# Second copies of the split keys by transfers inside SBUF, and VectorE's splits one step behind ScalarE's

## The reference, cut to what matters

```python
ks = partial_rope(ks, pos); kw = partial_rope(kw, pos)
s = einsum('bgrqd,bgkd->bgrqk', q, k) * HEAD_DIM ** -0.5      # k is ks, then kw
p = softmax(where(kpos <= qpos, s, -inf)); o = einsum('bgrqk,bgkd->bgrqd', p, v)
o_n = g[..., 0:1] * o_c + g[..., 1:2] * o_s + g[..., 2:3] * o_w
```

## Time and profile before

| | us |
|---|---|
| median of 3 runs | 2821.78 (2821.71 to 2824.16) |
| profiled execution, its own time | 2825.9 |
| its span, first to last instruction | 2824.1 |
| PE busy in the span | 2725.4 (97%) |
| DVE busy | 1525.5 (54%) |
| ACT busy | 1156.0 (41%) |
| POOL busy | 229.0 (8%) |

### The profile page before, as it was taken

One profiled execution on the slowest core, in us unless ns is written; L12 is line 12 of the kernel. 1 busy time (PEld: TensorE's weight loads), 2 busy tenths in 40 slices (PEclk: granted clock), 3 DMA queues, 4 the chain that ended last, 5 costly groups with the idle time before them and its releaser, 6 DMA issues.

```text
span 2824.1 us, 34777 instructions
## 1 busy us (share of the span) xinstructions
PE 2725.4 (97%) x13497; PEld 2246.0 (80%) x13497; DVE 1525.5 (54%) x2678; ACT 1156.0 (41%) x2076; POOL 229.0 (8%) x322
## 2 busy tenths in 40 slices
PE   8899999999999999989999999999989899999997
PEld 7778888887788888767778888888768788888886
DVE  5756444466564344576766653343667665643333
ACT  3654222236542222455654442242465654342331
POOL 4500000004000000011121000000010221000000
PEclk9999999999999999999999999999999999999999
DMA  4103333321033333321311233333213211323332
GB/s 125 50 23 94 97 97 97 97 84 56 23 94 97 97 97 98 86 67 53 105 53 46 90 97 97 97 97 98 82 50 90 75 46 60 104 91 97 97 97 75
DMA packets 186358, 231.40 MB, mean 82 GB/s; under 512 B 11874, under 2 KB 140356, under 8 KB 186196
## 3 DMA queue, kind: packets, MB, share of 16 engines
q1 hardware_dynamic: 184500, 225.95, 26.3%
q0 software_dynamic: 976, 1.32, 0.3%
q10 hardware_dynamic: 720, 1.92, 0.2%
HBM read 227.05 MB, written 2.11 MB: 81 GB/s over the span
## 4 chain that ended last, share of the span: by engine, by line
PE 79%; DVE 11%; ACT 5%; issue 4%; DMA 0%; POOL 0%; ACTq 0%; DVEq 0%; SPq 0%
PE bank L646 23%; PE bank L647 23%; PE bank L648 23%; DVE Wl L2192 2%; ACT Wh L1470 2%; PE bank L906 1%; PE bank L851 1%; DVE STT L2506 1%; PE bank L927 1%; PE bank L969 1%; PE bank L970 1%; PE bank L928 1%; PE bank L1163 1%; DVE KAl L2240 1%; ACT P L1667 1%
## 5 line engine op out<-in xcount | busy, mean ns | idle before, releaser
L2192 DVE TENSOR_TENSOR Wl<-RAW,Wh 128x1024 fp32r<-128x1024 f32 (+3 forms) x434 | 512.7, 1204 | 397.6 <-ACT Wh L1470 396.9
L1470 ACT ACTIVATE Wh<-RAW 128x1024 fp32r<-128x1024 f32 (+3 forms) x434 | 437.7, 1032 | 408.4 <-PE bank L648 406.4
L646 PE MATMUL bank<-Hh,Wh 128*128 128x512 f32 (+1 forms) x1104 | 448.5, 406 | 7.1 <-DVE Wl L2192 5.8
L648 PE MATMUL bank<-Hh,Wl 128*128 128x512 f32 (+1 forms) x1104 | 433.4, 393 | 0.0
L647 PE MATMUL bank<-Hl,Wh 128*128 128x512 f32 (+1 forms) x1104 | 432.9, 392 | 0.0
L646 PE MATMUL bank<-HA,Wh 128*128 128x512 f32 x704 | 274.2, 390 | 0.0
L647 PE MATMUL bank<-HA,Wh 128*128 128x512 f32 x704 | 273.9, 389 | 0.0
L648 PE MATMUL bank<-HA,Wl 128*128 128x512 f32 x704 | 273.9, 389 | 0.0
L646 PEld LDWEIGHTS bank<-Hh,Wh 128*128 128x128 f32 (+1 forms) x1104 | 207.9, 188 | 49.9 <-DVE Wl L2192 7.1
L648 PEld LDWEIGHTS bank<-Hh,Wl 128*128 128x128 f32 (+1 forms) x1104 | 207.1, 188 | 46.4
L647 PEld LDWEIGHTS bank<-Hl,Wh 128*128 128x128 f32 (+1 forms) x1104 | 207.6, 188 | 36.7
(11 more groups left out here) (398 smaller groups left out, 4749.2 us busy)
## 6 DMA issues: line engine op xcount, KB each, us to landing
RAW<-in_w_up_dram SPq DMA_DIRECT2D x108, 512.0 KB, 3.7
RAW<-in_w_down_dram SPq DMA_DIRECT2D x108, 512.0 KB, 3.7
RAW<-in_w_in_dram SPq DMA_DIRECT2D x90, 512.0 KB, 3.6
RAW<-in_w_gate_dram SPq DMA_DIRECT2D x44, 512.0 KB, 3.7
RAW<-in_w_out_dram SPq DMA_DIRECT2D x28, 512.0 KB, 3.7
RAW<-in_cmp_w_dram SPq DMA_DIRECT2D x16, 512.0 KB, 3.9
RAW<-in_w_o_fox_dram SPq DMA_DIRECT2D x8, 512.0 KB, 4.0
RAW<-in_w_o_nsa_dram SPq DMA_DIRECT2D x8, 512.0 KB, 3.4
```

Source lines behind the costliest of these rows:

```text
L646: pe.matmul(o, sh, mh, start=first, stop=False)
L648: return pe.matmul(o, sl, mh, start=False, stop=last)
L1470: sc.activation(M.Wh[:, v % NHL, 0:n], M.RAW[:, v % NRAW, 0:n], ACT.Copy).then_inc(G.w_hi, 1)
L2192: ve.tensor_tensor(M.Wl[:, v % NRAW, 0:n], M.RAW[:, v % NRAW, 0:n], M.Wh[:, v % NHL, 0:n].bitcast(F32), ALU.subtract).then_inc(G.w_lo, 1)
```

## The change

For the four query tiles the work is the same, but counted on a new semaphore (`heads_hi`), and DVE's part stands one step later: the first of its two instructions in the step after ACT's first. For the key tiles ACT and DVE write partitions 0 to 63 alone, DVE again one step later. POOL, between the scalings of the two attentions, waits for each half and issues four DMAs per layer that copy partitions 0 to 63 of `KSh` and `KSl` to 64 to 127 (64 partitions of 4 KB each, 256 KB a DMA). PE waits for all four before it starts the softmax pipeline.

```diff
# PE, nsa_side
             yield from idle(5)
+            pe.wait_ge(G.nsa_twice, 64 * (l + 1))
             for j in range(2):
                 pe.wait_ge(*K.drained(f"nk{l} {j}"))
# ACT, heads_side
             if j < 4:
+                name = f"nq{l} {j}"
+                sc.wait_ge(*K.full(name))
                 for x in range(2):
-                    packed_q(M.QN[:, 2 * j + x, :], f"nq{l} {j}", x, 0.125)
+                    sc.activation(M.QN[0:64, 2 * j + x, :], M.bank[K.of(name)][64 * x:64 * x + 64, :], ACT.Copy, scale=0.125).then_inc(*heads_hi.up())
                     yield
             else:
-                packed_k([(M.KSh[:, j - 4, x, :], 1.0) for x in range(2)], f"nk{l} {j - 4}")
+                name = f"nk{l} {j - 4}"
+                sc.wait_ge(*K.full(name))
+                for x in range(2):
+                    sc.activation(M.KSh[0:64, j - 4, x, :], M.bank[K.of(name)][64 * x:64 * x + 64, :], ACT.Copy).then_inc(*heads_hi.up())
+                K.points["nsa keys hi", l, j - 4] = heads_hi.now()
                 yield
# DVE, heads_side
             yield
+            yield
             if j < 4:
                 name = f"nq{l} {j}"
                 for x in range(2):
-                    i = packed_q(M.QN[:, 2 * j + x, :], name, x, 0.125)
+                    q = M.QN[:, 2 * j + x, :]
+                    ve.wait_ge(*heads_hi.due())
+                    i = ve.scalar_tensor_tensor(q[64:128, :], M.bank[K.of(name)][64 * x:64 * x + 64, :], 0.125, q[0:64, :].bitcast(F32), ALU.mult, ALU.subtract)
                     if x:
                         i.then_inc(*K.empties(name))
                     yield
             else:
-                packed_k([(M.KSh[:, j - 4, x, :], M.KSl[:, j - 4, x, :], None) for x in range(2)], f"nk{l} {j - 4}")
-                yield
-            yield
+                name = f"nk{l} {j - 4}"
+                for x in range(2):
+                    ve.wait_ge(*heads_hi.due())
+                    i = ve.tensor_tensor(M.KSl[0:64, j - 4, x, :], M.bank[K.of(name)][64 * x:64 * x + 64, :], M.KSh[0:64, j - 4, x, :].bitcast(F32), ALU.subtract)
+                i.then_inc(*K.empties(name))
+                yield
# POOL, between the two attentions
         normalise(fox_bundles(l), lambda t, g, h: M.ONE[:, 0:1])
+        for j in range(2):
+            gp.wait_ge(*K.points["nsa keys hi", l, j])
+            gp.dma_start(M.KSh[64:128, j, :, :], M.KSh[0:64, j, :, :]).then_inc(G.nsa_twice, 16)
+            gp.wait_ge(*K.drained(f"nk{l} {j}"))
+            gp.dma_start(M.KSl[64:128, j, :, :], M.KSl[0:64, j, :, :]).then_inc(G.nsa_twice, 16)
         gp.wait_ge(*K.drained(f"fgt{l}"))
```

More of the change, by code:

```diff
@@ L401, in __init__ @@
         self.xf = sem("blocks_split")
+        self.heads_hi = sem("nsa_upper_parts_made")
+        self.nsa_twice = sem("nsa_keys_copied")
         self.rq = sem("nsa_q_turned")
@@ L1455, in scalar_program @@
     cut, unit = [0], [0]
-    hi, sq, ex = Count(G.part_hi), Count(G.sq), Count(G.ex)
+    hi, sq, ex, heads_hi = Count(G.part_hi), Count(G.sq), Count(G.ex), Count(G.heads_hi)
     mx, a_mul, a_sq = Count(G.mx), Count(G.a_mul), Count(G.a_sq)
@@ L2177, in vector_program @@
     cut, unit = [0], [0]
-    own, hi = Count(G.v_own), Count(G.part_hi)
+    own, hi, heads_hi = Count(G.v_own), Count(G.part_hi), Count(G.heads_hi)
     a_lo, silu, sig, fox_lo = Count(G.a_lo), Count(G.silu), Count(G.sig), Count(G.fox_lo)
```

## The result

| | before | after |
|---|---|---|
| median | 2824.16 us (5 runs) | 2834.06 us (5 runs) |
| ratio, 95% interval | | 1.0038 [1.0023, 1.0053] |
| profiled execution, its own time; span | 2825.9; 2824.1 | 2834.06; 2832.3 |
| PE waiting for the last transfer, both layers | none | 10.2 us |

The change makes the kernel 9.9 us slower. The forecast was +3.2 us, 2825.0 with a range to 2830.0; it was wrong. Of the distance from 2825.0 to 2834.06, 2.4 us lie in the base (the three runs shown ahead had a median of 2821.78), 6.7 in the change.

What follows compares the result with a forecast made beforehand. PE, busy 97% of the span, was taken to bound the kernel. A later first score (+1.6 us in both layers) and one clock fall (+1.6) made +3.2 on the median 2821.78: 2825.0 us, range 2819.0 to 2830.0.

Steps and rivals of the forecast that it cites:

- What bounds: Whole kernel: PE, busy 97% of the span, bounds it; better order can take under 2 us from it in both layers.
- removed copies: Key tiles: ACT saves 2.4 us and DVE 2.8 us a layer, hidden by PE wherever it is not waiting for them.
- the step behind: Splitting stretch: DVE takes `M` earlier, `Wl` starts 0.7 us earlier at 1370.2, keys end at 1375.4, 2.2 us earlier.
- POOL's issues: POOL's idle gap before the scalings: four issues a layer of 0.54 us, 2.2 us together, costing nothing by themselves.
- PE's readiness: Before the first score: PE ready at 1376.86, the 0.40 us wait for `Wl` being gone.
- The transfer: Last key copy: issued at 1375.5, landing 3.2 us later at 1378.7, with ends of 1.8 and 4.8 us.
- rival 1: Before the first score: the last transfer lands late, at 4.8 us costing +8.0 us, 2829.8; chance 0.22.
- The clock: After PE's new 1.9 us wait: one fall of the granted clock in the two layers, +1.6 us.
- Rivals 2 and 3: 2: last copy lands early, at 1.8 us, -4.4 us, chance 0.15; 3: DVE is no earlier, +9.2 us, chance 0.05.

Runs made afterwards that it cites:

- e5: The change without its transfers: DVE's splits one step later, ACT and DVE writing both halves as in the kernel before; 2824.02 us, 1.0003 to before.
- e1: The changed kernel plus a fifth transfer per layer, repeating the last copy after all four landed, PE waiting for it; 2840.58 us, one run.
- e7: The changed kernel with the two weight loads beside the copies held until all four copies landed; 2827.79 us, 1.0012 to the kernel before.
- e8: The changed kernel with only the first key tile copied by transfer and the weight loads held until those copies landed; 2823.49 us, 0.9997 to before.

## Why the prediction was wrong, point by point

- **What bounds, removed copies, the step behind: right.** `M` stands before the second `QN`, `Wl` starts at 1370.2 on the clock of before, as worked out, and its wait on PE is gone. DVE is done with the keys at 1375.3 (1375.4 forecast). e5 shows no gain from this half alone.
- **POOL's issues: right.** 0.52 to 0.59 us each, for 0.54.
- **PE's readiness: 0.5 us earlier** than 1376.86 (1375.15 + 1.2 = 1376.35). Of this 0.17 is the wait for `HT`, which went with the one for `Wl`. It lengthens the wait and costs nothing.
- **The transfer: this is the step that failed.** "From issue to landing ... I take 3.2" took the bytes of one copy at a rate, from rows with at most one neighbour in flight. Alone a copy takes 2.8, the last of four without the loads 3.0 to 3.9, and with the loads 6.24 and 5.29. I had seen the loads, and set them aside in rival 1: they "are landing and the third transfer has a lead of 2 us". At the last issue, 1374.41, only the first had landed (1369.22 + 4.3 = 1373.5); `w_o_fox`, issued at 1370.58, landed 6.9 us later, at 1377.5, since the copies delay it in turn. And the lead of the third transfer, 2.1 us, was worth nothing, for it took 6.2 us itself. A rough sum of engine time, worked out afterwards, says it: from the first copy's issue at 1368.90 four copies (5.6) and two loads (3.5) fill the engines for 9.1 us, to 1378.0. About 1 us is left of the load issued at 1366.95 (3.6 to its landing), and 1.4 is the part of a flight that is no engine time (2.8 alone less 1.4): 1380.4, for 1380.65 measured. In the second layer, from 2194.30, the same sum gives 2205.8 for 2205.10, so it holds to 0.7 us.
- **Rival 1 was the case, beyond its end.** Its formula with the measured landings: (6.24 - 2.4) + (5.29 - 2.4) + 3.2 = 9.9 us; the two stretches cost 9.3, and the medians differ by 9.9. By parts, the first score starts 4.2 and 3.2 us later, for 4.0 and 3.1 by the formula, and 1.2 and 0.7 are lost behind it, for 1.4 each. So its mechanism and about its price held, though the agreement to a tenth is luck; its 4.8 and its chance of 0.22 did not hold. I had taken 4.8, the slowest load of the stretch beside other loads, as the upper end for a stretch to which the change itself adds 1.05 MB.
- **The clock: as in rival 1**, a fall in both layers (1381 us: 0.50; in the second from 2203 on, while PE still waits), where the forecast charged one. By the account above they cost less than the 1.6 a layer charged, 1.1 and 0.6: in the second layer the fall behind the second transposes, which the forecast left as it is, is gone.
- **Rivals 2 and 3** had nothing for them: no landing under 2.8 us, and DVE was earlier.

## What to carry to other kernels

A transfer inside SBUF is not free of HBM traffic: here it shared the DMA engines with weight loads, so its landing is worked out from all that is in flight from its issue on, in engine time, and not from its own bytes. A few microseconds of flight ahead of an in-order engine's wait must lie under work of that engine that triggers no transfer of its own. And a side pipeline's start step is worth a trial by itself: here it gave what the change did not.

## What the runs showed that I had not expected

- Copies between partitions of SBUF take more engine time for a byte than weight loads: alone 1.27 us of all sixteen for 256 KB (e1, 206 GB/s), beside the loads 1.4, against 1.7 us for 512 KB (304 GB/s).
- The delay is mutual: the 512 KB load of `w_o_fox` took 6.9 us beside the copies, for 4.8 before.
- Without the loads, the four copies of e7's first layer, issued 2.9, 0.5 and 2.1 us apart, took 2.9, 2.8, 3.7 and 3.9 us, one alone 2.8: the later two pay about 1 us for each other and the second.
- Of PE's waits ahead of the first score in the change and its variants, all fifteen of 3.1 to 8.7 us have a fall of the granted clock to 0.50 in them or right behind; of the seven from 1.7 to 2.6 us one has (e8, 1.80).
